# Two chained transformer blocks on one core: every second up panel multiplied as a 2 x 2 block product with seven half-size products instead of eight

## The chip, the cores and the metric

The kernel runs on one core of a Trainium2 chip. The metric is the device time of one execution in microseconds, the median over runs. A core has TensorE (matrix multiplication, called PE in the profile), VectorE (DVE), ScalarE (ACT), GpSimd (POOL) and SyncE (SP, which only issues DMAs here). They run their own programs in order and wait for each other by semaphores. TensorE writes into PSUM, which has eight banks of 512 float32 columns; VectorE and ScalarE read it from there.

## What is computed

The reference chains two blocks on x of 512 tokens and 1024 features. The first is a mixer (long convolutions and an mLSTM), cross attention and a perceptron with a squared relu. The second has two layers, each with a mixer and a gated perceptron. What the change touches are the three perceptrons (cut to that):

```python
h = h + jnp.square(jax.nn.relu(_rms_norm(h, norm_ff_g[l]) @ ff_w1[l])) @ ff_w2[l]      # "ff": 1024 -> 4096 -> 1024
...
def swiglu(x, w_gate, w_up, w_down):
    return (jax.nn.silu(x @ w_gate) * (x @ w_up)) @ w_down                             # "glu0", "glu1": 1024 -> 2816 -> 1024
```

All is float32. The kernel gets near that precision with float16 multiplications: each operand is split into a high part (rounded to float16) and a low part (the rest, as float16), and a product is the sum of high x high, high x low and low x high.

## The kernel before

Features lie on the 128 partitions and tokens in the columns. Weights come in panels of 128 x 2048 float32 (1 MB; for an up or gate matrix 8 row tiles by 256 output features). SyncE loads panel g into W[g % 2] as soon as panel g - 2 is split (semaphore panel_low). `split` runs on two engines: ScalarE writes the high half (128 x 2048, L1240), then VectorE the low half (L1822), into W16, the two homes in W_PARTS that TensorE reads in turn. `earlier` and `released` say which panel must have been multiplied before its home is written again.

A product on TensorE (`product`, L383 to L385) is three matmuls. A perceptron (`mlp`) has these stages:

- Head: the first two panels, in halves of 256 tokens (`half_panels`), while the normalization before it still works on the second half of the tokens. Their homes are in ARENA. Two more panels are split meanwhile (head_panel + 2 and + 3).
- Up panels: each later panel is 2 tiles of 128 features by 512 tokens; a tile is 8 products of 512 columns in one bank of the ring A (psum_a, four banks). In ff the panels are ("up", 2) to ("up", 15), in the glus ("gate", j) and ("up", j) for j = 1 to 10, in turn.
- After each tile ScalarE reads the bank into TS with relu or silu (`first_tiles`, L1325), VectorE makes the hidden tile in GF (`hidden`, a square at L2007 in ff, gate times up at L2004 in the glus), ScalarE its high part (`hidden_high`, L1334) and GpSimd its low part (L2644). GF and TS have room for two panels, so a tile of panel j waits for hidden_low of panel j - 2.
- Down panels: first the lower 512 output features (512 columns each), then the upper ones in halves of 256 tokens.

The ring B (psum_b, three banks) serves the norm sums and is idle during the up panels. GpSimd also multiplies x by a constant after a norm (`rescale`) for the residual.

Of the kernel before, what the change touches and what calls it, by code (L numbers as in the profile page):

```python
# [8 lines left out]
P = 128  # L9
T = 512  # L10
# [21 lines left out]
for _name, _n in ([(n, 8) for n in ("norm_mix", "norm_x", "norm_mem", "norm_ff", "final", "mix_g0", "mix_g1", "mix_b0",  # L32
# [9 lines left out]
              ("gla01", 128), ("selcol", 127), ("halfcol", 128), ("groupback", 512), ("rope_cos", 512),  # L42
              ("rope_sin", 512), ("filt_z", 512), ("decay", 2048), ("decay_b0", 512)]
# [5 lines left out]
SMALL_W1, SMALL_W2, SMALL_W3, SMALL_GATE, N_SMALL = 0, 64, 128, 2176, 2432  # L49

# [43 lines left out]
def build(nc, x_in, mem_in, weights, params, small_w, const, dft, y_out):  # L94
    with ExitStack() as ctx:
# [119 lines left out]
        G16 = parts(m.take(32 * T), 32, T)  # L215
        TS = m.take(4, T)
        GF = m.take(4, T)
        NT = Arena(8192).take(8, T)

# [7 lines left out]
        HOMES = [W16[:, 0], W16[:, 1], spare16[:, 0], spare16[:, 1], mix16w[:, 0], mix16w[:, 1], last16]  # L227
        IN_ARENA, IN_MIX, IN_LAST = (2, 3), (4, 5), 6
# [84 lines left out]
        class Mlp:  # L313


            def __init__(self, name, groups, gated, norm, next_norm):
                self.name, self.groups, self.gated, self.norm, self.next_norm = name, groups, gated, norm, next_norm
                self.ups = ("gate", "up") if gated else ("up",)
                self.head = (("gate", 0), ("up", 0)) if gated else (("up", 0), ("up", 1))
                self.later_ups = [(what, j) for j in range(groups) for what in self.ups if (what, j) not in self.head]  # L320
# [6 lines left out]
        FF = Mlp("ff", FF_GROUPS, False, "ff", "final")  # L327
        GLU0 = Mlp("glu0", GLU_GROUPS, True, "ln_mix0", "ln_ffn0")
        GLU1 = Mlp("glu1", GLU_GROUPS, True, "ln_mix1", "ln_ffn1")
# [29 lines left out]
        def _(pe):  # L359
# [21 lines left out]
            def product(out, left, right, first, last):  # L381

                nc.tensor.matmul(out, left(0), right(0), start=first, stop=False)  # L383
                nc.tensor.matmul(out, left(0), right(1), start=False, stop=False)  # L384
                return nc.tensor.matmul(out, left(1), right(0), start=False, stop=last)  # L385
# [499 lines left out]
            def mlp(M):  # L885
                half_panels([(M.name,) + key for key in M.head],
                            [lambda m, half, key=key: (M.name,) + key + (m, half) for key in M.head], IN_ARENA, U16,
                            wait=low_halves(M.norm), **second_sums(M.norm))
                for key in M.later_ups:
                    w, g = panel()  # L890
                    panel_of[(M.name,) + key] = g
                    w = w.rearrange("p l (k c) -> p l k c", k=KT)
                    for m in range(2):
                        bank = reuse(A, (M.name,) + key + (m,))
# [21 lines left out]
                for n, (key, tiles) in enumerate(M.low_steps):  # L916
                    w, g = weights(key, tiles)
                    final = n == len(M.low_steps) - 1
                    for m in range(4):
                        if n == 0:  # L920
                            banks[m] = reuse(A, (M.name, "y", m))
                        for i, kt in enumerate(tiles):
                            if m == 0:
                                pe.wait_ge(sem(f"hidden_low_{M.name}"), kt + 1)
                            last = product(banks[m][:, :], lambda l: w[:, l, i, m * P:(m + 1) * P], lambda l: G16[:, l, kt, :],
                                           n + i == 0, final and i == len(tiles) - 1)
                        if final:
                            last.then_inc(A.done, 1)
                    if not final:
                        step_done(g, last)  # L930
                    elif key != "both":
                        released[g] = A.done, A.n

# [273 lines left out]
        def _(act):  # L1207
# [37 lines left out]

            def high(ready, n, out, src, signal, bias=None):
# [1703 lines left out]
```

## Time and profile before

| | |
|---|---|
| time before, median of 3 runs (lowest, highest) | 1993.16 us (1988.92, 1994.02) |
| span of the profiled execution | 1992.6 us |
| its own time beside the span | none is shown; the span is the first to the last instruction |
| mean granted TensorE clock | 0.995 of full speed |
| TensorE busy / weight loads | 1958.3 us (98%) / 1185.2 us |
| VectorE, ScalarE, GpSimd busy | 934.0 us, 732.8 us, 345.4 us |
| chain that ended last | PE 91%, DVE 5%, the rest 1% each |
| DMA | 179.66 MB, mean 90 GB/s |

The busy time of TensorE is the union of its matmuls, whose ends are modelled (they overlap), so rates are read from the distance between starts. The chain that ended last is followed back from the last instruction to what released each.

### The profile page before, as it was taken

What the parts mean: (1) busy time and instruction counts of PE and PEld (TensorE: products, weight loads), DVE (VectorE), ACT (ScalarE), POOL (GpSimd) and SP (SyncE); (2) the same over time, 40 slices, a digit from 0 to 9 for tenths busy, and PEclk for the clock granted to TensorE, in tenths of its full rate; (3) what the DMA queues carried; (4) which work ended last, traced back from release to release, by engine and by line L of the source; (5) the groups of instructions that cost most, each with busy time, mean ns of one, the idle gap of its engine ahead of it and who ended that gap; (6) DMA issues with size and microseconds to landing.
All of it is one profiled execution on the core that took longest, in us unless ns stands there. A gap on an engine that the chain in (4) does not pass through costs nothing.

```text
span 1992.6 us, 27298 instructions
## 1 busy us (share of the span) xinstructions
PE 1958.3 (98%) x11532; PEld 1185.2 (59%) x11532; DVE 934.0 (47%) x1254; ACT 732.8 (37%) x1173; POOL 345.4 (17%) x355
## 2 busy tenths in 40 slices
PE   8999999999999999999999999999999999999997
PEld 5655655757664444885577444448775585444476
DVE  6666776655543322245755222223555663222224
ACT  6344311444343331144534322213455543223213
POOL 1011111410131210033024211200500124212001
PEclk9999999999999999999999999999999999999999
DMA  7221200233322333322221223333121023322331
GB/s 249 84 84 52 77 22 22 95 118 106 106 79 93 104 106 106 105 87 100 70 106 64 95 96 106 106 106 128 43 75 53 24 83 106 106 102 93 101 106 43
DMA packets 28228, 179.66 MB, mean 90 GB/s; under 512 B 2960, under 2 KB 7184, under 8 KB 7184
## 3 DMA queue, kind: packets, MB, share of 16 engines
q1 hardware_dynamic: 27312, 170.93, 24.9%
q10 hardware_dynamic: 512, 4.94, 0.7%
q0 software_dynamic: 288, 2.10, 0.3%
q8 instruction: 91, 1.49, 0.3%
q14 instruction: 25, 0.20, 0.0%
HBM read 175.86 MB, written 2.10 MB: 89 GB/s over the span
## 4 chain that ended last, share of the span: by engine, by line
PE 91%; DVE 5%; ACT 1%; DMA 1%; issue 1%; POOL 1%; SPq 0%; ACTq 0%; DVEq 0%
PE psum_a L383 26%; PE psum_a L384 26%; PE psum_a L385 26%; PE psum_b L520 2%; PE psum_a L726 2%; PE psum_a L662 1%; PE psum_a L737 1%; DMA W<-weights 1%; PE psum_b L639 1%; DVE ARENA L1841 1%; PE psum_a L704 1%; PE psum_a L853 1%; PE psum_b L1065 1%; PE psum_a L1019 0%; PE psum_a L1084 0%
## 5 line engine op out<-in xcount | busy, mean ns | idle before, releaser
L1822 DVE SCALAR_TENSOR_TENSOR W_PARTS<-W,W_PARTS 128x2048 f16<-128x2048 f32 x138 | 316.1, 2294 | 575.3 <-ACT W_PARTS L1240 575.1
L383 PE MATMUL psum_a<-U,W_PARTS 128*128 128x512 f16 (+1 forms) x1240 | 466.0, 376 | 2.1 <-DVE U L1836 2.1
L384 PE MATMUL psum_a<-U,W_PARTS 128*128 128x512 f16 (+1 forms) x1240 | 465.9, 376 | 0.0
L385 PE MATMUL psum_a<-U,W_PARTS 128*128 128x512 f16 (+1 forms) x1240 | 465.8, 376 | 0.0
L1240 ACT ACTIVATE W_PARTS<-W 128x2048 f16<-128x2048 f32 x138 | 262.4, 1906 | 441.9 <-PE psum_a L385 440.1
L383 PE MATMUL psum_a<-ARENA,W_PARTS 128*128 128x256 f16 (+1 forms) x860 | 268.1, 312 | 4.1 <-DVE ARENA L2339 2.3
L385 PE MATMUL psum_a<-ARENA,W_PARTS 128*128 128x256 f16 (+1 forms) x860 | 268.0, 312 | 0.0
L384 PE MATMUL psum_a<-ARENA,W_PARTS 128*128 128x256 f16 (+1 forms) x860 | 268.0, 312 | 0.0
L383 PEld LDWEIGHTS psum_a<-U,W_PARTS 128*128 128x128 f16 x1240 | 121.5, 98 | 147.5 <-issue 5.2
L385 PEld LDWEIGHTS psum_a<-U,W_PARTS 128*128 128x128 f16 x1240 | 121.5, 98 | 141.8 <-issue 1.1
L384 PEld LDWEIGHTS psum_a<-U,W_PARTS 128*128 128x128 f16 x1240 | 121.5, 98 | 141.3 <-issue 3.7
L2644 POOL TENSOR_TENSOR ARENA<-ARENA 128x512 f16<-128x512 f32 x76 | 118.2, 1575 | 452.7 <-ACT ARENA L1334 452.7
L1325 ACT ACTIVATE ARENA<-psum_a 128x512 f32<-128x512 f32 (+1 forms) x84 | 45.5, 552 | 186.1 <-PE psum_a L385 186.0
L383 PEld LDWEIGHTS psum_a<-ARENA,W_PARTS 128*128 128x128 f16 x860 | 84.2, 98 | 48.8 <-issue 2.8
L385 PEld LDWEIGHTS psum_a<-ARENA,W_PARTS 128*128 128x128 f16 x860 | 84.2, 98 | 43.4
L384 PEld LDWEIGHTS psum_a<-ARENA,W_PARTS 128*128 128x128 f16 x860 | 84.2, 98 | 43.3
L383 PE MATMUL psum_a<-MIX,W_PARTS 128*128 128x256 f16 (+1 forms) x288 | 92.2, 320 | 0.5 <-DVE MIX L1908 0.5
L384 PE MATMUL psum_a<-MIX,W_PARTS 128*128 128x256 f16 (+1 forms) x288 | 92.1, 320 | 0.0
L385 PE MATMUL psum_a<-MIX,W_PARTS 128*128 128x256 f16 (+1 forms) x288 | 92.1, 320 | 0.0
L2004 DVE SCALAR_TENSOR_TENSOR ARENA<-psum_a,ARENA 128x512 f32<-128x512 f32 (+1 forms) x48 | 30.8, 646 | 101.0 <-PE psum_a L385 101.0
L2601 POOL TENSOR_TENSOR SQ<-SQ 128x256 f32<-128x256 f32 x16 | 18.2, 1155 | 280.4 <-ACT SQ L1223 280.3
L1334 ACT ACTIVATE ARENA<-ARENA 128x512 f16<-128x512 f32 x76 | 44.7, 620 | 52.4 <-DVE ARENA L2007 46.8
(317 smaller groups left out, 2950.1 us busy)
## 6 DMA issues: line engine op xcount, KB each, us to landing
W<-weights SPq DMA_DIRECT2D x159, 1024.0 KB, 4.8
CON<-const ACTq DMA_DIRECT2D x1, 3071.5 KB, 11.5
X<-x_in SPq DMA_DIRECT2D x4, 256.0 KB, 3.9
X<-x_in SPq DMA_DIRECT2D x1, 1024.0 KB, 7.9
U<-dft POOLq DMA_DIRECT2D x1, 1024.0 KB, 5.3
ARENA<-dft POOLq DMA_DIRECT2D x1, 1024.0 KB, 5.2
U<-mem_in ACTq DMA_DIRECT2D x1, 1024.0 KB, 4.8
y_out<-U SPq DMA_DIRECT2D x2, 512.0 KB, 2.9
```

The costliest lines, as they stand in the source:

```text
L383: nc.tensor.matmul(out, left(0), right(0), start=first, stop=False)
L384: nc.tensor.matmul(out, left(0), right(1), start=False, stop=False)
L385: return nc.tensor.matmul(out, left(1), right(0), start=False, stop=last)
L520: last = nc.tensor.matmul(bank[:, 0:HALF], ones, square_tile(kt), start=kt == 0, stop=kt == KT - step)
L639: nc.tensor.matmul(bank[:, :], QK[:, 4 + h, j * P:(j + 1) * P], QK[:, h, :], start=True, stop=True).then_inc(B.done, 1)
L726: last = nc.tensor.matmul(bank[:, :], FDFT[:, part, odd, n, kt * P:(kt + 1) * P], sources[part][:, 2 * odd + n, :], start=n == 0, stop=n == 1)
L1240: nc.scalar.activation(HOMES[home_of[g]][:, 0, :], W[g % 2][:, :], ACT.Copy, scale=W_SCALE).then_inc(sem("panel_high"), 1)
L1325: nc.scalar.activation(TS[:, 2 * (j % 2) + m, cols], A.bank(key)[:, 0:cols.stop - cols.start], ACT.Silu if M.gated else ACT.Relu, scale=DE ...
L1334: nc.scalar.activation(G16[:, 0, 2 * j + m, :], GF[:, 2 * (j % 2) + m, :], ACT.Copy).then_inc(sem(f"hidden_high_{M.name}"), 1)
L1822: nc.vector.scalar_tensor_tensor(out=home[:, 1, :], in0=W[g % 2][:, :], scalar=W_SCALE, in1=home[:, 0, :], op0=ALU.mult, op1=ALU.subtract) ...
L2004: nc.vector.scalar_tensor_tensor(out=g, in0=A.bank(up)[:, 0:n], scalar=DESCALE, in1=ts, op0=ALU.mult, op1=ALU.mult).then_inc(A.freed_sem(u ...
L2644: nc.gpsimd.tensor_tensor(G16[:, 1, n, :], GF[:, n % 4, :], G16[:, 0, n, :], ALU.subtract)\
```

## The change

In `mlp` the later up panels go in pairs: a plain panel, multiplied as before, and one by seven products. In ff the pairs are (2, 3), (4, 5) to (14, 15), 7 in all; in each glu (gate j, up j) for j = 1 to 10. For the second of a pair the panel is taken as 2 x 2 blocks A (output tile m by even or odd row tiles), and the input as 2 x 2 blocks (even or odd row tiles by first or second half of the tokens). The seven products are a form of Strassen's scheme. Each is 4 x 3 matmuls of 128x256, into 256 columns of a psum_b bank:

- q1 (A11 x B11), q6, q7 and q4 accumulate one after another in psum_b0; q5 and q3 in psum_b2; q2 (A12 x B21) in psum_b1.
- The order is q1, q5, q2, q6, q3 (`first_five`), then the next plain panel's tile 0, q7 (`sixth`), its tile 1, q4 (`seventh`), and the next q1. After the last pair q7 and q4 stand behind the first two down tiles.
- Between the accumulations the running sums are read: q1, q5 and q1 + q6 by ScalarE (`read_part` 0, 1, 2 into SQ), and with them VectorE adds the three quarters of the two output tiles (`add_part` 0 after q2, 1 after q3, 2 after q7). The fourth quarter is psum_b0 after q4, read by ScalarE in ff (`tile_21`) and by VectorE in the glus (in `finish`).

The combined operands are made on chip. Once for each perceptron VectorE makes four combinations of the input, 128x1024 each (`v_made`), split into high (ScalarE, `v_high`) and low parts (VectorE, `v_low`). For each panel it makes four sums of 128x512 (`block_sums`), and the seven blocks are split in three steps (`raw` 1024 columns, `sums` 1536, `rest` 1024), instead of one split of 2048. The host orders the columns of those panels by blocks. The second panel that was split under the head is now one of these, so one is left there; the glu heads' homes move from 12288 to 1536 in ARENA, where the blocks now need room; and `rescale` starts after v_made.

The diff, cut:

```diff
             def mlp(M):
+                def one_of_seven(name):
+                    block, right = source[name]
+                    opens = name in ("q1", "q5", "q2")
+                    for i in range(4):
+                        last = product(out_of[name][:, 0:HALF], lambda l: M.blocks[:, l, block, i, :], lambda l: right(l)[:, i, :],
+                                       opens and i == 0, i == 3, not opens)
+                    last.then_inc(sem("seven_done"), 1)
+
+                def first_five(key):
...
+                    pe.wait_ge(sem("blocks_low"), 2 * n + 1)
+                    if n:
+                        pe.wait_ge(sem("tile_21"), n)
+                    one_of_seven("q1")
+                    pe.wait_ge(sem("blocks_low"), 2 * n + 2)
+                    pe.wait_ge(sem("v_low"), 4 * MLPS[M.norm] + 4)
+                    if n:
+                        pe.wait_ge(sem("tile_added"), 3 * n - 1)
+                    one_of_seven("q5")
+                    one_of_seven("q2")
+                    pe.wait_ge(sem("part_read"), 3 * n + 1)
+                    one_of_seven("q6")
+                    pe.wait_ge(sem("part_read"), 3 * n + 2)
+                    one_of_seven("q3")
+
+                def sixth(key):
+                    pe.wait_ge(sem("panel_low"), panel_of[(M.name,) + key] + 1)
+                    pe.wait_ge(sem("part_read"), 3 * M.seven[key] + 3)
+                    one_of_seven("q7")
+
+                def seventh(key):
+                    pe.wait_ge(sem("tile_added"), 3 * M.seven[key] + 3)
+                    one_of_seven("q4")
...
-                for key in M.later_ups:
+                for plain, seven in M.pairs:
                     w, g = panel()
...
                         last.then_inc(A.done, 1)
+                        if before:
+                            (sixth, seventh)[m](before)
                     released[g] = A.done, A.n
+                    first_five(seven)
+                    before = seven
```

ScalarE's `mlp`:

```diff
                 split(head_panel(M.norm, 2))
-                split(head_panel(M.norm, 3))
                 for j in range(1 if M.gated else 2):
                     first_tiles(M, j, 1)
+                v_high(M)
+                for j in range(1 if M.gated else 2):
                     hidden_high(M, j)
-                for j in range(1 if M.gated else 2, M.groups):
-                    first_tiles(M, j)
-                    used_panels(M, [(what, j) for what in M.ups])
-                    hidden_high(M, j)
+                before = None
+                for plain, seven in M.pairs:
+                    raw_high(M, seven)
+                    sums_high(M, seven)
+                    if before:
+                        hidden_high(M, before[1], (0,))
+                        if not M.gated:
+                            tile_21(M, before)
+                    plain_tile(M, plain, 0)
+                    rest_high(M, seven)
+                    if before:
+                        hidden_high(M, before[1], (1,))
+                    split(panel_of[(M.name,) + seven] + 1)
+                    plain_tile(M, plain, 1)
+                    for i in range(3):
+                        read_part(M, seven, i)
+                    if not M.gated:
+                        hidden_high(M, plain[1])
+                    before = seven
```

VectorE's `mlp` (`rest_high` on ScalarE waits for q4 of the panel before, `raw_high` for its q3):

```diff
                 split(head_panel(M.norm, 2))
-                split(head_panel(M.norm, 3))
+                v_made(M, X if M.gated else NT)
...
+                v_low(M)
+                block_sums(M, M.pairs[0][1])
+                before = None
+                for n, (plain, seven) in enumerate(M.pairs):
+                    if before:
+                        add_part(M, before, 1)
+                    raw_low(M, seven)
+                    if before:
+                        finish(M, before, 0)
+                    sums_low(M, seven)
+                    if before:
+                        add_part(M, before, 2)
+                        finish(M, before, 1)
+                    rest_low(M, seven)
+                    split(panel_of[(M.name,) + seven] + 1)
+                    if not M.gated:
+                        hidden(plain[1])
+                    add_part(M, seven, 0)
+                    if n + 1 < len(M.pairs):
+                        block_sums(M, M.pairs[n + 1][1])
+                    before = seven
```

On TensorE in ff, at the turn from one panel to the next. Before, the first matmuls of each bank are these, each followed by 23 more into the same bank, down three panels:

```order
L383 MATMUL psum_a2<-U,W_PARTS 128x512 [waits a_free2,panel_low]
...
L383 MATMUL psum_a3<-U,W_PARTS 128x512 [waits a_free3]
...
L383 MATMUL psum_a0<-U,W_PARTS 128x512 [waits a_free0,panel_low]
...
L383 MATMUL psum_a1<-U,W_PARTS 128x512 [waits a_free1]
...
L383 MATMUL psum_a2<-U,W_PARTS 128x512 [waits a_free2,panel_low]
```

Now, at the same place, from the second plain panel on (MIX holds the input's combinations and CON the blocks; the rows are a plain tile, q7, a plain tile, the end and the start of q4, q1, q5, q6 and q3):

```order
L422 MATMUL psum_a0<-U,W_PARTS 128x512 [waits a_free0,panel_low]
...
L422 MATMUL psum_b0<-MIX,CON 128x256 [waits part_read,panel_low]
...
L422 MATMUL psum_a1<-U,W_PARTS 128x512 [waits a_free1]
...
L422 MATMUL psum_b0<-MIX,CON 128x256 [waits tile_added]
...
L424 MATMUL psum_b0<-MIX,CON 128x256
L422 MATMUL psum_b0<-U,CON 128x256 [waits tile_21,blocks_low]
...
L422 MATMUL psum_b2<-MIX,CON 128x256 [waits tile_added,v_low,blocks_low]
...
L422 MATMUL psum_b0<-MIX,CON 128x256 [waits part_read]
...
L422 MATMUL psum_b2<-U,CON 128x256 [waits part_read]
```

Between tiles that waited for a bank four tiles old stand now products that wait for reads of the bank just written: q1 (tile_21) directly behind q4, and q6 (part_read).

ScalarE's queue for one pair in ff (the rows after hidden_high of the plain panel: raw_high, sums_high, hidden_high, tile_21 at L1487, a plain tile, rest_high, hidden_high, the next panel's split, a plain tile, and the three read_part at L1381); before, a panel had two tiles, one split and two hidden_high:

```order
L1353 ACTIVATE CON<-W0 128x1024 [waits seven_done,panel_landed0]
L1359 ACTIVATE CON<-SMALL 128x1536 [waits block_sum]
L1475 ACTIVATE ARENA<-ARENA 128x512 [waits relu_squared]
L1487 ACTIVATE ARENA<-psum_b0 128x256 [waits seven_done]
L1481 ACTIVATE ARENA<-psum_a0 128x512 [waits a_done]
L1368 ACTIVATE CON<-W0 128x1024 [waits block_sum,seven_done]
L1475 ACTIVATE ARENA<-ARENA 128x512 [waits relu_squared]
L1341 ACTIVATE W_PARTS<-W1 128x2048 [waits a_done,panel_landed1]
L1481 ACTIVATE ARENA<-psum_a1 128x512 [waits a_done]
L1381 ACTIVATE SQ<-psum_b0 128x256 [waits seven_done]
L1381 ACTIVATE SQ<-psum_b2 128x256 [waits seven_done]
L1381 ACTIVATE SQ<-psum_b0 128x256 [waits seven_done]
```

The copy of q1 stands five operations behind tile_21, all of them behind q4 of the panel before.

VectorE under the head of glu0. Before, two splits follow each other between the hidden tiles of the head's halves:

```order
L2004 SCALAR_TENSOR_TENSOR ARENA<-psum_a2,ARENA 128x256 [waits a_done,a_free0]
L1822 SCALAR_TENSOR_TENSOR W_PARTS<-W0,W_PARTS 128x2048 [waits panel_high]
L1822 SCALAR_TENSOR_TENSOR W_PARTS<-W1,W_PARTS 128x2048 [waits panel_high]
L2004 SCALAR_TENSOR_TENSOR ARENA<-psum_a1,ARENA 128x256 [waits a_done,a_free3]
L2004 SCALAR_TENSOR_TENSOR ARENA<-psum_a2,ARENA 128x256 [waits a_done,a_free0]
```

Now:

```order
L1996 SCALAR_TENSOR_TENSOR W_PARTS<-W0,W_PARTS 128x2048 [waits panel_high]
L2038 TENSOR_TENSOR ARENA<-X 128x1024 [waits gained_ln_mix0,high_ln_mix0]
L2040 SCALAR_TENSOR_TENSOR ARENA<-ARENA,X 128x1024 [waits v_made]
L2043 SCALAR_TENSOR_TENSOR ARENA<-ARENA,X 128x1024 [waits v_made]
L2047 SCALAR_TENSOR_TENSOR ARENA<-X,PAR 128x256 x4
L2281 SCALAR_TENSOR_TENSOR ARENA<-psum_a3,ARENA 128x256 [waits a_done,a_free1]
L2281 SCALAR_TENSOR_TENSOR ARENA<-psum_a0,ARENA 128x256 [waits a_done,a_free2]
L2059 SCALAR_TENSOR_TENSOR MIX<-ARENA,MIX 128x1024 [waits v_made,v_high] x4
L2005 TENSOR_TENSOR ARENA<-W1 128x512 [waits panel_landed1]
L2007 TENSOR_TENSOR ARENA<-ARENA,W1 128x512 [waits block_sum]
L2009 TENSOR_TENSOR ARENA<-ARENA,W1 128x512 [waits block_sum]
L2010 TENSOR_TENSOR W1<-W1 128x512
```

One split has gone, and v_made, v_low and the first panel's sums stand before the first raw_low, for which q1 waits.

## Rows read from the trace of the kernel before

**Rows 1.** The page, busy time, share of the span and instructions.
```profile
PE 1958.3 (98%) x11532; PEld 1185.2 (59%) x11532; DVE 934.0 (47%) x1254; ACT 732.8 (37%) x1173; POOL 345.4 (17%) x355
```
**Rows 2.** Stage table: up panels of ff and glu0, and the kernel's end.
```profile
core 0: us, PE busy (x) PEld busy (x) DVE busy (x) ACT busy (x) POOL busy (x), PEclk, DMA share, GB/s
578.90:720.50 141.60, 141.60 (x657) 64.19 (x656) 48.95 (x42) 57.14 (x69) 30.18 (x27) 1.00 0.29 98
1086.40:1293.00 206.60, 206.60 (x959) 93.71 (x958) 59.68 (x40) 58.83 (x59) 38.83 (x21) 1.00 0.30 102
...
1978.00:1992.00 14.00, 4.29 (x19) 3.15 (x17) 8.20 (x18) 6.83 (x18) 0.00 (x0) 0.85 0.37 125
```
**Rows 3.** Order in time (start, duration, us), ff, matmuls of 512 columns: 15 rows.
```profile
639.79 0.38 PE L383 MATMUL psum_a<-U,W_PARTS 128*128 128x512 f16 x1
...
642.81 0.38 PE L385 MATMUL psum_a<-U,W_PARTS 128*128 128x512 f16 x1
```
**Rows 4.** The same, matmuls of 256 columns: 26 rows, and their readers.
```profile
899.84 0.27 PE L384 MATMUL psum_a<-U,MIX 128*128 128x256 f16 x1
...
901.25 0.27 PE L385 MATMUL psum_a<-U,MIX 128*128 128x256 f16 x1
...
901.56 0.66 ACT L1273 ACTIVATE ARENA<-psum_a 128x256 f32<-128x256 f32 x2
...
902.55 0.39 ACT L1273 ACTIVATE ARENA<-psum_a 128x256 f32<-128x256 f32 x1 [0.33 <-PE psum_a L385]
902.57 0.27 PE L385 MATMUL psum_a<-U,MIX 128*128 128x256 f16 x1
```
**Rows 5.** Line L2004: durations in ns, least, median, most.
```profile
L2004 DVE SCALAR_TENSOR_TENSOR ARENA<-psum_a,ARENA x48: 406/691/694, 1069.1 to 1857.4; 128x512 f32<-128x512 f32 x40, 128x256 f32<-128x256 f32 x8
```
**Rows 6.** Order in time where TensorE waited for L2339 (0.42 us each).
```profile
399.49 0.76 DVE L2339 SCALAR_TENSOR_TENSOR ARENA<-psum_a,ARENA 128x256 f16<-128x256 f32 x2
400.03 0.10 PEld L383 LDWEIGHTS psum_a<-ARENA,W_PARTS 128*128 128x128 f16 x1 [1.21 <-issue]
400.06 0.27 PE L383 MATMUL psum_a<-ARENA,W_PARTS 128*128 128x256 f16 x1 [0.96 <-DVE ARENA L2339]
```
**Rows 7.** Order in time, head of ff: the two prepared splits.
```profile
561.56 3.71 ACT L1240 ACTIVATE W_PARTS<-W 128x2048 f16<-128x2048 f32 x2
...
563.50 4.49 DVE L1822 SCALAR_TENSOR_TENSOR W_PARTS<-W,W_PARTS 128x2048 f16<-128x2048 f32 x2 [2.83 <-ACT W_PARTS L1240]
```
**Rows 8.** Order in time, ScalarE in a panel of ff.
```profile
641.28 0.60 ACT L1325 ACTIVATE ARENA<-psum_a 128x512 f32<-128x512 f32 x1 [3.28 <-PE psum_a L385]
641.78 1.90 ACT L1240 ACTIVATE W_PARTS<-W 128x2048 f16<-128x2048 f32 x1
646.64 1.23 ACT L1334 ACTIVATE ARENA<-ARENA 128x512 f16<-128x512 f32 x2 [2.96 <-DVE ARENA L2007]
```
**Rows 9.** DMA issues, median us to landing.
```profile
W<-weights SPq DMA_DIRECT2D x159, 1024.0 KB, 4.8
```
**Rows 10.** Head of glu0: order in time, and durations of L2667 in ns.
```profile
1039.54 2.77 DVE L1902 TENSOR_TENSOR X<-X,MU 128x256 f32<-128x256 f32 x8
...
1071.18 4.49 DVE L1822 SCALAR_TENSOR_TENSOR W_PARTS<-W,W_PARTS 128x2048 f16<-128x2048 f32 x2 [1.31 <-ACT W_PARTS L1240]
...
1076.47 0.42 DVE L2004 SCALAR_TENSOR_TENSOR ARENA<-psum_a,ARENA 128x256 f32<-128x256 f32 x1 [0.46 <-PE psum_a L385]
...
1071.36 4.58 POOL L2667 TENSOR_SCALAR X<-X,PAR 128x256 f32<-128x256 f32 x1
...
L2667 POOL TENSOR_SCALAR X<-X,PAR x24: 474/476/4579, 1070.1 to 1656.9; 128x256 f32<-128x256 f32 x24
```
**Rows 11.** Order in time, head of ff: hidden tiles, GpSimd, the next reader.
```profile
567.91 1.42 DVE L2007 TENSOR_TENSOR ARENA<-ARENA 128x256 f32<-128x256 f32 x4
570.49 2.66 DVE L2007 TENSOR_TENSOR ARENA<-ARENA 128x256 f32<-128x256 f32 x4 [1.15 <-ACT ARENA L1325]
...
569.74 2.46 POOL L2644 TENSOR_TENSOR ARENA<-ARENA 128x512 f16<-128x512 f32 x2 [7.28 <-ACT ARENA L1334]
...
579.12 0.60 ACT L1325 ACTIVATE ARENA<-psum_a 128x512 f32<-128x512 f32 x1 [4.58 <-PE psum_a L385]
```

More of the change, by code:

```diff
@@ L49 @@
 SMALL_W1, SMALL_W2, SMALL_W3, SMALL_GATE, N_SMALL = 0, 64, 128, 2176, 2432
+BLOCK = 512
+A11, A12, S1, S2, S4, A22, S3 = range(7)
+V5, V6, V4, V7 = range(4)
+PRODUCTS = ("q1", "q5", "q2", "q6", "q3", "q7", "q4")
 F32 = mybir.dt.float32
@@ L313, in build, with __init__ @@
         class Mlp:
-            def __init__(self, name, groups, gated, norm, next_norm):
+            def __init__(self, name, groups, gated, norm, next_norm, hidden, blocks, sums, v32, homes, seven_before):
                 self.name, self.groups, self.gated, self.norm, self.next_norm = name, groups, gated, norm, next_norm
+                self.hidden, self.blocks, self.sums, self.v32, self.homes = hidden, blocks, sums, v32, homes
+                if gated:
+                    self.pairs = [(("gate", j), ("up", j)) for j in range(1, groups)]
+                else:
+                    self.pairs = [(("up", j), ("up", j + 1)) for j in range(2, groups, 2)]
+                self.seven = {b: seven_before + n for n, (_, b) in enumerate(self.pairs)}
                 self.ups = ("gate", "up") if gated else ("up",)
                 self.head = (("gate", 0), ("up", 0)) if gated else (("up", 0), ("up", 1))
-                self.later_ups = [(what, j) for j in range(groups) for what in self.ups if (what, j) not in self.head]
                 chunks = [(c, range(4 * c, 4 * c + 4)) for c in range(groups // 2)]
@@ L379, in panel, with product @@
                 return HOMES[home], g
[L381 to L385, printed above, removed]
+            def product(out, left, right, first, last, goes_on=False):
+                nc.tensor.matmul(out, left(0), right(0), start=first, stop=False, skip_group_check=goes_on)
+                nc.tensor.matmul(out, left(0), right(1), start=False, stop=False, skip_group_check=goes_on)
+                return nc.tensor.matmul(out, left(1), right(0), start=False, stop=last, skip_group_check=goes_on)
             def project_panel(name, q, rhs, width=T, first_wait=None, inside=None, after=None, home=None):
@@ L885, in mlp @@
             def mlp(M):
+                G16 = M.hidden
                 half_panels([(M.name,) + key for key in M.head],
-                            [lambda m, half, key=key: (M.name,) + key + (m, half) for key in M.head], IN_ARENA, U16,
+                            [lambda m, half, key=key: (M.name,) + key + (m, half) for key in M.head], M.homes, U16,
                             wait=low_halves(M.norm), **second_sums(M.norm))
-                for key in M.later_ups:
+                even, odd, first, second = slice(0, KT, 2), slice(1, KT, 2), *HALVES
@@ L928, in mlp @@
                             last.then_inc(A.done, 1)
+                        if n == 0 and m == 0:
+                            sixth(before)
+                        elif n == 0 and m == 1:
+                            seventh(before)
                     if not final:
@@ L932, in mlp @@
                         released[g] = A.done, A.n
+                pe.wait_ge(sem("tile_21"), M.seven[before] + 1)
+                pe.wait_ge(sem("tile_added"), 3 * M.seven[before] + 3)
                 wide = {}
@@ new lines, in block_low, with raw_low @@
+            def block_low(M, first, end, src, high, n, signal):
+                flat = lambda l: M.blocks[:, l, first:end].rearrange("p b k c -> p (b k c)")
+                dve.wait_ge(sem(high), n)
+                nc.vector.scalar_tensor_tensor(out=flat(1), in0=src, scalar=W_SCALE, in1=flat(0), op0=ALU.mult, op1=ALU.subtract)\
+                    .then_inc(sem(signal), 1)
+            def raw_low(M, key):
+                n, g = M.seven[key], panel_of[(M.name,) + key]
+                block_low(M, A11, A12 + 1, W[g % 2][:, 0:2 * BLOCK], "blocks_high", 2 * n + 1, "blocks_low")
@@ L2783, in _down_panels, with _by_blocks, _seven_from @@
     return low + both + high
+def _by_blocks(panel):
+    w = panel.reshape(P, 4, 2, 2, P)
+    return _np.concatenate([w[:, :, k, m].reshape(P, BLOCK) for m, k in ((0, 0), (0, 1), (1, 1), (1, 0))], 1)
+def _seven_from(panels, first):
+    return [_by_blocks(w) if n >= first and n % 2 else w for n, w in enumerate(panels)]
 def _swiglu_panels(gate, up, down):
-    return [w for pair in zip(_panels_k8(gate), _panels_k8(up)) for w in pair] + _down_panels(down)
+    return _seven_from([w for pair in zip(_panels_k8(gate), _panels_k8(up)) for w in pair], 3) + _down_panels(down)
 def _weight_stream(a):
```

223 lines of the change are left out of this document (191 added, 32 removed).

## The prediction

> **What bounds the kernel now.** I read the page first, for the engine that sets the end; then stage tables for the three stretches of up and gate panels, where the change lies; then the order in time inside them. TensorE is busy 98% of the span [rows 1]. In the stretch of a perceptron in which whole panels of 512 columns follow one another (ff and glu0 are shown, glu1 is like glu0), its busy time equals the stretch to the last digit, while VectorE and ScalarE are busy less than half of it [rows 2]. Nobody is waited for there: only work taken from TensorE shortens the stretch, and whatever makes TensorE wait lengthens it by the full wait.
>
> **What the change removes.** A plain panel is 48 matmuls of 512 columns. They start 0.2157 us apart (14 steps in 3.02 us, [rows 3]): 10.35 us. A panel by seven products is 7 x 12 = 84 matmuls of 256 columns. The new ones are not in the trace, but others of that width are, and start 0.1092 us apart (25 steps in 2.73 us, [rows 4]): 9.17 us. Saved: 1.18 us a panel and, for 7 + 10 + 10 = 27 panels, **31.9 us**. Not an eighth of 27 x 10.35 = 279 (34.9), since each matmul has a small cost of its own that is now paid more often.
>
> **What it adds on TensorE's path, in the steady pairs.** I put t = 0 at the end of q4's slot, the last product of the previous seven, which accumulates in psum_b0.
>
> *q4 to q1.* The next product, q1, overwrites psum_b0, so it waits for whoever reads q4's result (tile_21), and nothing stands between them. A reader starts 0.31 us after the last 256-column matmul has started (901.25 to 901.56, [rows 4]), 0.20 after its slot. A VectorE read of 256 columns from PSUM takes 0.41 at least [rows 5]. From the end of such an operation (399.49 + 0.42) to the next matmul of a TensorE that waited for it are 0.14 us (400.06, [rows 6]). Together 0.75 us. ScalarE reads q4 in the ff perceptron. It falls in every pair but the first of each perceptron, 24 times: **18.0 us**. One of its 256-column reads alone takes 0.39, two in a row 0.66, so the second adds 0.27 [rows 4]. Bounds: 0.51 (0.20, a read of 0.27 and hardly any release) to 0.86, so 12 to 21 us.
>
> *q1 to q6.* q6 accumulates on q1 in the same bank and waits until ScalarE has copied q1 (read_part 0). Between them stand q5 and q2. With the wait above q2's slot ends at 0.75 + 36 x 0.1092 = 4.68. The copy stands in ScalarE's queue behind work that itself waits for q4. Spacings there: 2048 columns 1.81 (two in 3.71, [rows 7]), 512 columns 0.50 to 0.55 (641.28 to 641.78, and two in 1.23, [rows 8]), 256 columns 0.27; on the line between 512 and 2048, 1024 columns cost 0.96. In glu0 and glu1 it is: start 0.20, rest_high 0.96, hidden_high 0.55, the next panel's split 1.81, plain_tile 0.50, the copy 0.39: 4.41, and 4.55 with the release. That is 0.13 before TensorE arrives: nothing is lost, narrowly. In ff tile_21 (0.27) and a plain_tile (0.50) stand ahead as well: 5.32, so TensorE waits 0.64 us in 6 pairs: **3.8 us**. Bounds: 0, if one of these is shorter; 0.5 more in each of the 24 pairs (12 us), if each of the queued operations costs its duration instead of its spacing.
>
> *Covered edits.* The other waits have room. A panel lands 4.8 us after its issue [rows 9]; rest_low ends at 2.5 in glu (3.3 in ff), so the next blocks land at 7.5 to 8 and their first four sums run in 7.5 to 11.5. raw_low ends by 13 and sums_low by 15.5, against a need at 20.3 or later. add_part 2 is wanted by q4 at 19, and ready at 14.5 to 16. The plain panel's low half is written at 5.9 to 6.7 and wanted at 7.3 to 8. VectorE's new operations per pair (3584 columns of low halves, four sums, three partial tiles) bring its work to about 13 of some 20 us. If any of it is late, q4's wait for add_part 2 comes first: that cover is 3 to 4 us.
>
> **A port that two engines want.** VectorE operations with two operands in SBUF and GpSimd operations lengthen each other here: GpSimd's 128x256 operation, 0.476 us in the median, took 4.58 while two splits ran on VectorE [rows 10], and four VectorE multiplications took 2.66 us beside GpSimd against 1.42 alone [rows 11]. In a steady pair GpSimd needs 4 x 1.2 us (two in 2.46, [rows 11]) and VectorE some 11 us with two such operands: 16 of 20, so it holds. It costs in the start below. The Trainium skill has this as a rule (SBUF — State Buffer, "Who interferes with whom"): a VectorE instruction with two SBUF inputs contends with a GpSimd instruction that reads SBUF, and whoever issues first keeps the port for the whole instruction. The rows agree. Without that rule, with no delay of the sums, the start would cost 5.5 us less in all.
>
> **The start of each perceptron.** Before, the second prepared panel is split under the head and nobody waits. Now v_made, v_low, the sums and raw_low stand on VectorE before q1. In glu0, in the times of the old trace: the first split ends at 1073.45 (half of the two from 1071.18, [rows 10]); three 1024-column operations at 1.15 and four of 256 at 0.4 end at 1078.5 (1024 columns from 0.346 a 256-column operation, eight in 2.77, and 2.25 a split); two hidden tiles 1079.25; v_low four times 1.13 with a first wait of 0.3 gives 1084.1. The sums are chained by semaphores, 0.65 each, and GpSimd's rescale, which now runs there, enters the two gaps at 0.65 on average: the third ends 1087.35, the fourth 1088.0, raw_low 1089.1. TensorE ends the head at 1076.27 (the reader starts 1076.47, [rows 10]) and the plain panel at 1086.6: it waits 2.6 us for q1, and 0.4 more for sums_low before q5. That is 3.0, and 3.0 in glu1. In ff the head ends at 568.55 (the reader at 579.12, less 0.2 and one panel, [rows 11]). The split ends 565.75 [rows 7], v_made 570.35, eight hidden halves 573.05, v_low 577.6, the sums, with GpSimd's 1.2 us tiles in both gaps, 582.6, raw_low 583.7; TensorE's plain panel ends at 578.9: 4.8 + 0.4 = 5.2 us. Together **11.2 us**; without GpSimd in the gaps 5.7, with every operation held once 14.
>
> **Sum.** 31.9 - 18.0 - 3.8 - 11.2 = -1.1 us: the wins are spent. The profile's own span is 1992.6; no other time of that execution is shown, and the median of the runs is 1993.16, 0.6 above it. I take the median plus 0.8, **1994.0 us**.
>
> **Rivals.** A measurement of this kernel can tell some 0.3%, or 6 us.
> - *Faster.* The starts and q6's wait are hidden (ScalarE and VectorE as quick as their shortest rows, GpSimd kept out of the gaps) and the turnaround is 0.65: 31.9 - 15.6 - 2 = 14 us, 1979. For it: I priced 1024 columns by a line between other sizes, and three starts from one pattern. Against it: the turnaround is a chain of three rows. Half-way cases lie within 6 us. Chance beyond 6 us: 0.20.
> - *Slower: q6 waits in all 24 pairs.* The margin in glu is 0.13 us. If the five queued ScalarE operations cost 0.1 us more each, glu loses 18 x 0.37 = 6.7 and ff 3.0 more: 2004. It decides from about 0.3 us over the queue as a whole. Chance 0.18.
> - *Slower: VectorE is late.* If the port makes a pair's VectorE work longer than its 3 to 4 us of cover, q4 waits. One us in each of 24 pairs gives 2018. The 4 us in hand speak against it. Chance 0.06.
> - *The clock.* TensorE ran at 2.4 GHz (granted 1.00) in those stretches, and the grant fell only where it was busy 4.29 of 14 us (0.85, [rows 2]). New gaps of 0.75 in 20 us are far from that. If a fifth of the 27 pairs ran at 1.2 GHz, 5 x 20 = 100 us would be added: 2094. Chance 0.03. The Trainium skill warns of it (TensorE: Matmul & The Clock Gate, "A second HAM failure mode: psum-queue depth-cycling"): short idle moments between groups while PSUM banks are cycled made the clock alternate. No row here shows that.
> - *As summed*, within 6 us of no change: 0.53.
>
> **How the numbers follow.** Faster is the first rival, 0.20; slower the next three, 0.27; same 0.53. The range leaves out the far part of the faster case (below 1984), the late VectorE, the clock and the far part of the ScalarE case (above 2003), 2 in 10 together. The sum's own range, from the middle of its bounds, is 1987 to 1999.
>
> **What would show it.** In the profile after: (1) matmuls of the products 0.109 us apart, 84 in 9.17 us; (2) 24 gaps of 0.75 us on TensorE released by L1487 in ff and L2090 in glu; (3) gaps near 0.6 before q6 in ff, released by L1381, and none in glu; (4) 3 to 5 us of waiting in each start, released by L2016; (5) no waits for add_part or landing; (6) clock 1.00. I am wrong if (2) is under 0.5 or (4) under 1 us, or if (3) shows in glu.

## The result, and the profile after

The changed kernel takes 1997.13 us (median of 16 runs, 1994.36 to 1998.22) against 1992.38 us for the kernel before (16 runs beside it, 1988.89 to 1996.20). The ratio is 1.0018 with a 95% interval of 1.0011 to 1.0025: slower, by 2 to 5 us, and within the 0.3% that the prediction called no change. The forecast was 1994.0, which is 0.8 above the median that it started from; the measured difference is 3.6 us by the ratio and 4.7 by the medians. The profiled execution took 1997.98 us with a span of 1996.2; the span of before was 1992.6.

The busy line of the page, as [rows 1]:

```profile
PE 1936.5 (97%) x12504; PEld 1279.8 (64%) x12504; DVE 1137.3 (57%) x1547; ACT 805.4 (40%) x1313; POOL 377.2 (19%) x355
```

TensorE has 972 matmuls more, and its busy time is 22 us less. (It is not 31.9 less: the busy time also counts a modelled end at each new gap, and some matmuls ran at a lower clock, as shown below.) The span did not get shorter, so TensorE waits more. The stage table shows where, as [rows 2]; the rows are the start of ff, its second pair, the other five of ff, glu0 from its second pair on with the first down panels behind, and the kernel's end:

```profile
core 0: us, PE busy (x) PEld busy (x) DVE busy (x) ACT busy (x) POOL busy (x), PEclk, DMA share, GB/s
578.90:606.79 27.89, 22.14 (x132) 14.11 (x132) 20.78 (x19) 10.53 (x14) 9.32 (x6) 0.88 0.21 76
606.79:627.55 20.76, 19.86 (x132) 12.77 (x132) 14.14 (x15) 9.85 (x15) 6.35 (x4) 1.00 0.29 102
627.55:731.30 103.75, 99.33 (x661) 63.98 (x662) 67.29 (x71) 49.47 (x71) 33.93 (x21) 1.00 0.32 112
1115.70:1320.00 204.30, 198.88 (x1290) 125.61 (x1291) 108.01 (x124) 80.08 (x101) 34.54 (x19) 1.00 0.30 109
1977.86:1991.86 14.00, 7.64 (x29) 5.46 (x26) 8.79 (x20) 6.49 (x18) 0.00 (x0) 0.88 0.22 75
```

Before, TensorE's busy time equalled each such stretch. Now it lacks 0.90 of 20.76 us in a pair of ff, and the first row lacks 5.75 and ran at a granted clock of 0.88. (The busy time counts a matmul's modelled end, so a gap seen from start to start is a little longer.) TensorE's waits from the start of ff to the end of glu0 (us in total, times, longest):

```profile
PE psum_b L422 <- DVE CON L2016: 6.2, 1, 6.2
PE psum_b L422 <- DVE ARENA L2090: 5.5, 9, 0.6
PE psum_b L422 <- ACT ARENA L1487: 3.4, 6, 0.6
PE psum_b L422 <- ACT SQ L1381: 2.0, 6, 0.3
PE psum_b L422 <- DVE ARENA L2016: 1.9, 2, 1.5
```

The first is the start of ff and the last the start of glu0: q1 and q5 waiting for the first low halves. The second (glu0) and the third (ff) are q1 waiting for the reader of q4, the fourth is q6 waiting for the copy of q1. In the order in time (start, duration) they look like this, first in ff, then in glu0, then q6 in ff:

```profile
606.46 0.27 PE L424 MATMUL psum_b<-MIX,CON 128*128 128x256 f16 x1
606.77 0.38 ACT L1487 ACTIVATE ARENA<-psum_b 128x256 f32<-128x256 f32 x1 [7.21 <-PE psum_b L424]
607.30 0.27 PE L422 MATMUL psum_b<-U,CON 128*128 128x256 f16 x1 [0.56 <-ACT ARENA L1487]
...
1135.98 0.42 DVE L2090 SCALAR_TENSOR_TENSOR ARENA<-psum_b,ARENA 128x256 f32<-128x256 f32 x1 [5.33 <-PE psum_b L424]
1136.55 0.27 PE L422 MATMUL psum_b<-U,ARENA 128*128 128x256 f16 x1 [0.61 <-DVE ARENA L2090]
...
611.12 0.27 PE L424 MATMUL psum_b<-U,CON 128*128 128x256 f16 x1
611.72 0.28 PE L422 MATMUL psum_b<-MIX,CON 128*128 128x256 f16 x1 [0.33 <-ACT SQ L1381]
```

From 606.46 to 607.30 are 0.84 us where 0.109 would do: a gap of 0.73 (0.77 in the glus). From 611.12 to 611.72 are 0.60: 0.49. The start of ff, with VectorE, GpSimd and TensorE:

```profile
577.08 0.68 DVE L2005 TENSOR_TENSOR SMALL<-W 128x512 f32<-128x512 f32 x1
577.79 1.53 DVE L2007 TENSOR_TENSOR SMALL<-SMALL,W 128x512 f32<-128x512 f32 x1
...
580.80 1.64 DVE L2010 TENSOR_TENSOR W<-W 128x512 f32<-128x512 f32 x1
582.36 2.17 DVE L2016 SCALAR_TENSOR_TENSOR CON<-W,CON 128x1024 f16<-128x1024 f32 x1
...
572.94 10.52 POOL L2940 TENSOR_TENSOR ARENA<-ARENA 128x512 f16<-128x512 f32 x4 [11.13 <-ACT ARENA L1475]
...
578.06 0.38 PE L424 MATMUL psum_a<-U,W_PARTS 128*128 128x512 f16 x1
584.59 0.40 PE L422 MATMUL psum_b<-U,CON 128*128 128x256 f16 x1 [6.16 <-DVE CON L2016]
584.78 0.42 PE L423 MATMUL psum_b<-U,CON 128*128 128x256 f16 x1
```

TensorE waits 6.31 us for the first raw_low (from start to start 6.53, less 0.216 for a matmul of 512 columns); in each glu the same way 1.66 and then 0.55. Three of the four sums take 1.5 to 1.6 us where the first takes 0.68. And when TensorE goes on, 24 matmuls come 0.213 us apart (584.59 to 589.47), at a granted clock of 0.50, 1.2 GHz; only then they are 0.109 apart.

To compare kernels stage by stage I take the distance between the reciprocals (L1990, "RECIPROCAL RINV") of the second half of one norm and the first half of the next; a perceptron lies between them. Before and after: ff 321.35 and 329.17 us, glu0 337.18 and 334.49, glu1 337.17 and 334.49.

### The profile page after: what moved, and what is told of

Same layout as the page of the kernel before. It is cut to its first block, busy times and chain, and to the rows that moved or that the text cites. A ratio compares the mean times of both kernels' runs of the same rounds, so it can differ in the third digit from the quotient of the medians.

```text
span 1996.2 us, 29878 instructions
## 1 busy us (share of the span) xinstructions
PE 1936.5 (97%) x12504; PEld 1279.8 (64%) x12504; DVE 1137.3 (57%) x1547; ACT 805.4 (40%) x1313; POOL 377.2 (19%) x355
## 4 chain that ended last, share of the span: by engine, by line
PE 86%; DVE 8%; ACT 3%; issue 2%; DMA 1%; POOL 1%; SPq 0%; ACTq 0%; DVEq 0%
PE psum_a L422 21%; PE psum_a L424 21%; PE psum_a L423 21%; PE psum_b L422 4%; PE psum_b L424 4%; PE psum_b L423 4%; PE psum_b L559 2%; PE psum_a L765 2%; ACT W_PARTS L1341 1%; DVE ARENA L2118 1%; PE psum_a L701 1%; PE psum_a L776 1%; DMA W<-weights 1%; PE psum_b L678 1%; DVE MIX L2059 1%
## 5 line engine op out<-in xcount | busy, mean ns | idle before, releaser
L1996 DVE SCALAR_TENSOR_TENSOR W_PARTS<-W,W_PARTS 128x2048 f16<-128x2048 f32 x111 | 254.6, 2296 | 300.7 <-ACT W_PARTS L1341 300.6
L1341 ACT ACTIVATE W_PARTS<-W 128x2048 f16<-128x2048 f32 x111 | 211.0, 1904 | 277.6 <-PE psum_a L424 272.7
L422 PE MATMUL psum_a<-U,W_PARTS 128*128 128x512 f16 (+1 forms) x808 | 302.8, 375 | 1.6 <-DVE U L2113 1.6
L423 PE MATMUL psum_a<-U,W_PARTS 128*128 128x512 f16 (+1 forms) x808 | 302.4, 374 | 0.0
L424 PE MATMUL psum_a<-U,W_PARTS 128*128 128x512 f16 (+1 forms) x808 | 302.3, 374 | 0.0
L2940 POOL TENSOR_TENSOR ARENA<-ARENA 128x512 f16<-128x512 f32 x76 | 135.6, 1792 | 406.3 <-ACT ARENA L1475 406.3
L424 PEld LDWEIGHTS psum_a<-U,W_PARTS 128*128 128x128 f16 x808 | 79.4, 98 | 91.2 <-issue 1.4
L422 PEld LDWEIGHTS psum_a<-U,W_PARTS 128*128 128x128 f16 x808 | 79.4, 98 | 91.0 <-issue 5.2
L423 PEld LDWEIGHTS psum_a<-U,W_PARTS 128*128 128x128 f16 x808 | 79.4, 98 | 85.5 <-issue 4.0
L422 PE MATMUL psum_b<-MIX,ARENA 128*128 128x256 f16 x320 | 87.2, 273 | 0.8 <-DVE ARENA L2016 0.8
L423 PE MATMUL psum_b<-MIX,ARENA 128*128 128x256 f16 x320 | 87.2, 273 | 0.0
L424 PE MATMUL psum_b<-MIX,ARENA 128*128 128x256 f16 x320 | 87.2, 273 | 0.0
L422 PE MATMUL psum_b<-U,ARENA 128*128 128x256 f16 x240 | 65.4, 272 | 14.0 <-DVE ARENA L2090 11.0
```

The costliest lines, as they stand in the source:

```text
L1341: nc.scalar.activation(HOMES[home_of[g]][:, 0, :], W[g % 2][:, :], ACT.Copy, scale=W_SCALE).then_inc(sem("panel_high"), 1)
L1996: nc.vector.scalar_tensor_tensor(out=home[:, 1, :], in0=W[g % 2][:, :], scalar=W_SCALE, in1=home[:, 0, :], op0=ALU.mult, op1=ALU.subtract) ...
L2940: nc.gpsimd.tensor_tensor(M.hidden[:, 1, n, :], GF[:, n % 4, :], M.hidden[:, 0, n, :], ALU.subtract)\
```

## The experiments

All are edits of the changed kernel; the ratios are to the kernel before. The profiles decide here more than the medians: a perceptron that an edit leaves alone repeats to some hundredths of a microsecond, a median only to some 2 us. The medians of all seven fell by 1.3 to 3.3 us more, against the changed kernel's 1997.13, than their three perceptrons did; part of that is the clock in other stretches (see E3 and the sum at the end).

**E1, the bank behind q4 (e1_two_banks).**

```diff
+        def sum_bank(n):
+            return psum_den if n % 2 else psum_b[0]
...
-                    if n:
-                        pe.wait_ge(sem("tile_21"), n)
-                    one_of_seven("q1")
+                    if n > 1:
+                        pe.wait_ge(sem("tile_21"), n - 1)
+                    one_of_seven("q1", n)
```

> Edit: q1, q6, q7 and q4 of a panel go in turn into psum_b0 and into the eighth bank, which is idle in the perceptrons, so q1 waits for tile_21 of the panel before last. Time counted from the end of q4's slot. Theory (the wait behind q4 is real, but ScalarE's queue behind q4 stands right after it): the 24 gaps of 0.73 to 0.78 us before q1 go, and q6 then waits for the copy of q1, which still ends at 5.15 in ff and 4.45 in the glus, while TensorE arrives at 3.93. In ff the gap before q6 grows from 0.49 to about 1.2 and nothing is won; in each glu pair a gap of 0.5 comes up and 0.77 goes, 0.25 x 18 = 4.5 us. In all about 4.5 us less than the changed kernel, some 1992.5. Rival (the turnaround is a loss of its own, and the ScalarE queue has room): all 18.3 us come back, some 1979.

Measured: 1990.49 us (11 runs; before 1993.13; ratio 0.9989, 0.9980 to 0.9999). ff is 329.28, no shorter than 329.17; glu0 331.78, 2.71 less. TensorE in ff, the last matmul of q4, the first of q1, and then the turn from q2 to q6:

```profile
604.32 0.27 PE L428 MATMUL psum_b<-MIX,CON 128*128 128x256 f16 x1
604.42 0.27 PE L426 MATMUL psum_den<-U,CON 128*128 128x256 f16 x1
...
608.24 0.27 PE L428 MATMUL psum_b<-U,CON 128*128 128x256 f16 x1
609.57 0.28 PE L426 MATMUL psum_den<-MIX,CON 128*128 128x256 f16 x1 [1.06 <-ACT SQ L1386]
...
606.85 1.91 ACT L1346 ACTIVATE W_PARTS<-W 128x2048 f16<-128x2048 f32 x1
608.65 0.60 ACT L1486 ACTIVATE ARENA<-psum_a 128x512 f32<-128x512 f32 x1
609.12 0.39 ACT L1386 ACTIVATE SQ<-psum_den 128x256 f32<-128x256 f32 x1
```

The gap before q1 is gone (0.10 from start to start) and the one before q6 has grown from 0.49 to 1.22: the same 1.22 us, at another place. The copy (609.12) stands behind the split (606.85). In the glus 0.77 goes and 0.46 comes. So most of the 18.3 us of turnaround are not a loss of their own: they covered a wait for ScalarE's queue that shows as soon as they are gone.

**E2, the copy ahead of the split (e2_copy_first).** ScalarE:

```diff
                         hidden_high(M, before[1], (1,))
+                    read_part(M, seven, 0)
                     split(panel_of[(M.name,) + seven] + 1)
                     plain_tile(M, plain, 1)
-                    for i in range(3):
+                    for i in (1, 2):
```

> Edit: ScalarE copies q1 (read_part 0) before the split of the next plain panel, not after it and a plain tile. Theory: the 0.49 us gap before q6 goes in 6 pairs of ff, 2.9 us; in the glus there is none to take. The plain panel's split comes 0.38 later, ready 7.1 after q4's slot in ff against a need at 7.3, and 6.3 against 7.3 in the glus: no new wait. About 2.9 us less than the changed kernel, some 1994. Rival (the 0.49 us is made by something else, such as q5 or q2 waiting): no change. A price of the delayed split would show as a wait for panel_low before the plain panel.

Measured: 1992.89 us (11 runs; ratio 0.9998, 0.9989 to 1.0007). ff is 326.24, 2.93 less, and its gaps before q6 are gone; the glus are unchanged at 334.48. As expected to the tenth.

**E3, both (e3_both).** The diffs of E1 and E2 together.

> Edit: the two edits of the experiments with the alternating bank and the early copy together. Theory (two waits that cover one another): the gap before q1 (0.73 and 0.77) goes and none comes up before q6. The next bound is the plain panel's low half: in ff it is ready 7.1 us after q4's slot against a need at 6.55, so 0.6 comes back there, in the glus 6.3 against 6.55. Gain against the changed kernel: ff 6 x (0.73 + 0.49 - 0.6) = 3.8, glus 18 x 0.77 = 13.9, together 17.7 us, far more than the sum of the two apart (7.4); some 1979, under the kernel before by 13. Rival (the waits are independent): the sum of the two apart, whatever they give.

Measured: 1975.69 us (5 runs, 1974.19 to 1977.59; ratio 0.9916, 0.9902 to 0.9929). ff is 324.58 (4.59 less), glu0 327.57 (6.92 less), glu1 the same: 18.4 us, where the two alone gave 5.3 and 2.9. The turn from q4 to q1 in glu0 and the reader of q4:

```profile
1130.23 0.27 PE L428 MATMUL psum_b<-MIX,ARENA 128*128 128x256 f16 x1
1130.34 0.27 PE L426 MATMUL psum_den<-U,ARENA 128*128 128x256 f16 x1
...
1130.54 0.42 DVE L2096 SCALAR_TENSOR_TENSOR ARENA<-psum_b,ARENA 128x256 f32<-128x256 f32 x1 [4.55 <-PE psum_b L428]
```

The read now runs beside q1. In ff small gaps stay, 0.18 before q3 and 0.24 before the plain tile, where I had expected 0.6. The 17.7 expected became 18.4. The profiled span fell by more, 22.8: 1.7 of that is the clock in the last norm (below), and 2.6 lie in the mixer between glu0 and glu1, which the edit does not touch. There too the low clock fell on other matmuls: the granted clock was 0.50 from 1525.0 to 1531.6 in the changed kernel, and in E3 from 1504.5 to 1507.7 and from 1552.3 to 1555.5.

**E4, GpSimd held back in ff (e4_pool_held).** GpSimd:

```diff
                 pool.wait_ge(sem("v_made"), 4 * MLPS[M.norm] + 4)
+                if M is FF:
+                    pool.wait_ge(sem("blocks_low"), 2)
```

> Edit: in ff GpSimd starts its first hidden low halves only when the first raw and sums blocks are split, so that nothing of GpSimd runs beside the first block sums. Theory (port contention makes most of the start of ff): the sums take 0.7 us each and not 1.5, raw_low 1.2 and not 2.2, and q1 of the first pair comes some 4 us earlier: the wait falls from 6.3 to about 2 us. With the shorter idle the clock stays up, and the 2.5 us of half-speed matmuls go too. About 6.5 us less than the changed kernel, some 1990.5. Rival (the combinations and their low halves, v_made and v_low, are the start's cost): the wait stays above 5 us and the time within 1.5 us of the changed kernel.

Measured: 1990.19 us (12 runs; ratio 0.9983, 0.9974 to 0.9991). VectorE and TensorE in the start:

```profile
578.43 0.69 DVE L2007 TENSOR_TENSOR SMALL<-SMALL,W 128x512 f32<-128x512 f32 x1
...
579.76 0.68 DVE L2010 TENSOR_TENSOR W<-W 128x512 f32<-128x512 f32 x1
580.37 1.22 DVE L2016 SCALAR_TENSOR_TENSOR CON<-W,CON 128x1024 f16<-128x1024 f32 x1
...
581.64 0.40 PE L422 MATMUL psum_b<-U,CON 128*128 128x256 f16 x1 [2.57 <-DVE CON L2016]
```

The sums are back at 0.69 us and raw_low at 1.22, and the wait fell from 6.31 to 2.73 (2.95 from start to start): GpSimd's work beside them cost 3.58 us. The Trainium skill's rule (SBUF — State Buffer, "Who interferes with whom") fits with these rows. The second term of the expectation was wrong: the clock fell after the 2.73 us as well, for 16 matmuls and not for 24, so 0.85 came back and not 2.5. ff is 324.74, 4.43 less.

**E5, TensorE kept busy in the wait (e5_filler).**

```diff
                     released[g] = A.done, A.n
+                    if M is FF and not before:
+                        for n in range(27):
+                            nc.tensor.matmul(psum_b[1][:, :], w[:, 0, 0, 0:P], U16[:, 0, 0, :], start=True, stop=True)
                     first_five(seven)
```

> Edit: in ff, TensorE multiplies 27 more matmuls of 512 columns into an unused bank (results not used) between the first plain panel and q1, 5.8 us of the 6.3 us in which it waited for raw_low. Theory (TensorE's own idleness before q1 made the clock fall): q1 starts when it did, but its matmuls run 0.109 us apart and not 0.213, so that the 2.5 us lost after the wait come back; ff is shorter by 2.5 us. Rival (the clock falls there for another reason, or the 0.213 us come from a weight or operand port that is busy): the first 24 matmuls of q1 and q5 stay at 0.213 us apart and ff keeps its length.

Measured: 1992.83 us (11 runs; ratio 1.0003, 0.9994 to 1.0012), and ff 327.10, 2.07 less although TensorE does 27 matmuls more. The stretch behind the wait, in this kernel:

```profile
584.59:588.00 3.41, 3.00 (x26) 2.47 (x27) 3.41 (x4) 2.13 (x3) 0.00 (x0) 1.00 0.02 5
```

and in the changed kernel:

```profile
584.59:588.00 3.41, 3.41 (x17) 2.43 (x18) 3.41 (x3) 1.91 (x3) 0.00 (x0) 0.50 0.00 0
```

The granted clock is 1.00 against 0.50 with VectorE busy for all 3.41 us in both: it was TensorE's own idleness that lowered it. The 0.4 us short of 2.5 are a wait for sums_low (0.35) that q5 now meets, since q1 ends earlier.

**E6, two low halves later (e6_late_v).** VectorE's order and TensorE's waits:

```diff
-                v_low(M)
+                v_low(M, (V5, V6))
...
                     split(panel_of[(M.name,) + seven] + 1)
+                    if n == 0:
+                        v_low(M, (V4, V7))
...
-                    pe.wait_ge(sem("v_low"), 4 * MLPS[M.norm] + 4)
+                    pe.wait_ge(sem("v_low"), 4 * MLPS[M.norm] + 2)
```

(q7 now waits for all four.)

> Edit: of the four low halves of the input's combinations VectorE makes only the two that q5 and q6 use before the first block sums; the other two (q4's and q7's) come after the first split of the next plain panel. Theory (the starts are VectorE's queue, operation after operation): 2.3 us less ahead of raw_low. In each glu the waits of 1.65 and 0.55 us go, 2.2 each; in ff the wait before q1 falls by 2.3, perhaps more if the sums then escape some of GpSimd's tiles. Together 6.7 us or more less than the changed kernel, some 1990. Rival (the sums wait for something else, such as the panel's landing or GpSimd): the waits stay.

Measured: 1988.09 us (11 runs; ratio 0.9981, 0.9971 to 0.9990). The start of ff on TensorE:

```profile
578.15 0.38 PE L424 MATMUL psum_a<-U,W_PARTS 128*128 128x512 f16 x1
582.42 0.28 PE L422 MATMUL psum_b<-U,CON 128*128 128x256 f16 x1 [3.89 <-DVE CON L2017]
```

In the glus the waits at the start are gone (332.25 each, 2.24 less); in ff the wait is 4.05, 2.26 less, and ff is 326.14, 3.03 less (the other 0.7 are seven slow matmuls fewer). Together the three are 7.5 us shorter. What VectorE has queued before the first raw_low sets the starts: two operations fewer there shorten each by their length.

**E7, all four edits (e7_all_four).** E1, E2, E4 and E6 together.

> Edit: the alternating bank, the early copy, the held GpSimd and the late two low halves together. Theory: 17.7 to 21 us of steady gaps, 4.4 us of ff's start by GpSimd, and of what is left 2.2 in each glu and 2.3 in ff with its clock (0.9): some 1964 us, 1.5% under the kernel before, with a wait of under 1 us at each start, and TensorE at full clock through each perceptron's up panels. Rival (with GpSimd's first tiles later and VectorE's two low halves behind, the pairs that follow are late): waits for hidden_low, add_part or the plain panel's low half appear in the first two pairs and eat the gain of the starts; then some 1975.

Measured: 1966.93 us (4 runs, 1966.18 to 1968.44; ratio 0.9876, 0.9860 to 0.9892), 1.2% faster than the kernel before. glu0 and glu1 are 325.34 each, 9.2 less than the changed kernel and 11.8 less than before; ff 320.55, 8.6 less and 0.8 less. In ff the expectation's terms (3.8 of gaps, 4.4 and 3.2 of the start) make 11.4; it got 3 us less, by the rival's mechanism. VectorE, GpSimd and TensorE in ff:

```profile
582.52 3.29 DVE L2003 SCALAR_TENSOR_TENSOR W_PARTS<-W,W_PARTS 128x2048 f16<-128x2048 f32 x1 [0.99 <-ACT W_PARTS L1347]
585.74 4.27 DVE L2066 SCALAR_TENSOR_TENSOR MIX<-ARENA,MIX 128x1024 f16<-128x1024 f32 x2
...
580.53 8.39 POOL L2951 TENSOR_TENSOR ARENA<-ARENA 128x512 f16<-128x512 f32 x4 [18.67 <-DVE CON L2023]
...
599.61 0.41 DVE L2078 SCALAR_TENSOR_TENSOR ARENA<-psum_b,SQ 128x256 f32<-128x256 f32 x1
...
600.08 0.28 PE L426 MATMUL psum_b<-MIX,CON 128*128 128x256 f16 x1 [2.36 <-DVE ARENA L2078]
```

GpSimd's four tiles, held back, now lie beside the split (3.29, alone 2.29) and the two late low halves (4.27, 2.35 in E6); add_part 2 is late, and q4 waits 2.5 us for it, with 16 slow matmuls behind. The start's wait is down to 0.8. Part of what E4 and E6 won was only moved: q1 starts at 578.79 here, against 581.64 in E4 and 582.42 in E6, but add_part 2 stands at 599.61, against 599.64 and 599.24. In E4 and E6 alone TensorE came too late to wait for it.

## Why the prediction was right

It was right in its mechanism and close in its sum, with one term missing. By its steps:

- *Saving, 31.9.* Confirmed. The glu pairs take 20.30 us with a gap of 0.77; 19.53 without it is 10.35 + 9.17. Where nothing waits (E3, E7) it all arrives.
- *q4 to q1, 18.0.* Measured 6 x 0.73 + 18 x 0.77 = 18.3: the start 0.20 after the slot, the read 0.38 or 0.42, the release 0.14. The chain of three rows held. E1 shows what the prediction did not say: taken away alone, this wait gives back 2.7 us in each glu and nothing in ff, for the wait for ScalarE's queue comes up in its place.
- *q1 to q6, 3.8.* Measured 6 x 0.49 = 2.9 in ff and none in the glus; E2 took exactly that. Each queued operation costs its spacing, not its duration: from tile_21 to the copy the starts are 0.28, 0.48, 0.95, 0.52, 1.80 and 0.47 apart, priced at 0.27, 0.50, 0.96, 0.55, 1.81 and 0.50. By E1 the copy is ready 0.31 us before TensorE needs it in a glu (0.77 - 0.46), where I had 0.13: the rival in which q6 waits in all pairs was further off than its margin said.
- *Starts, 11.2.* Measured 6.31 + 2.2 + 2.2 = 10.7. The total is close because two errors cancel: ff was priced at 5.2 against 6.31, each glu at 3.0 against 2.2. In ff the contention also stretched raw_low (2.17 for 1.22), and q5's 0.4 did not appear beside the slow q1; in the glus rescale stretched the last three sums only to 0.77 to 0.88. E4 puts ff's contention at 3.6 us; with some 0.45 in each glu (an estimate from those three sums against 0.69 each) that is 4.5 where 5.5 was priced. E6 puts the rest at VectorE's queue.
- *The clock, 0.* This term was missing. The prediction looked for the clock in the pairs' gaps of 0.75 us, where it stayed at 1.00, and did not ask what a wait of 5 us at the start would do, though it had forecast that wait and had [rows 2] with a clock of 0.85 where TensorE idles. It also took those rows for the only place: the trace of before has another in the middle of dense work, with the clock at 0.50 for over 6 us behind one idle time of 1.78 us. The term costs 2.5 us here; E5 shows the cause. In before:

```profile
1518.25 0.40 PE L383 MATMUL psum_a<-ARENA,W_PARTS 128*64 128x512 f16 x1 [1.78 <-DVE MU L2454]
...
1520.20:1526.80 6.60, 6.60 (x20) 3.32 (x21) 1.28 (x5) 0.81 (x1) 0.00 (x0) 0.50 0.01 2
```

- *Covered edits.* No wait for a landing, add_part or the plain panel's low half in any steady pair: right. The cover is thin, as E7 shows where GpSimd's tiles fell on it.

Sum as measured: 31.9 - 18.3 - 2.9 - 10.7 - 2.5 = -2.5 us, against -1.1 forecast; the stages give 7.82 - 2.69 - 2.68 = +2.45. The errors of the three waits (0.3 too little, 0.9 and 0.5 too much) took back 1.1 of the missing 2.5, so a part of the closeness is luck. And the sum gives 1994.3 on 1993.16; the 0.8 taken in place of 1.1 has no reason given.

The profiled spans differ by 3.6. Besides the 2.45, 1.7 are the last norm: 12.42 us between its two reciprocals before, 14.11 after, with the granted clock at 1.00 and 0.88 in that stretch. That is not shown to be the change's: the stretch was 14.1 also in the profiles of E2 and E6, and 12.4 in those of E1, E3, E4, E5 and E7. The first mixer, ahead of ff, took 0.7 less than before, with the low clock at other places as well. What lowers the clock in the last norm in some executions stays open, as does what else the medians' 4.7 us holds.

## What to carry to other kernels

A product with an eighth fewer multiplications gives only what its operands' preparation and its accumulators' turnaround leave: here 32 us were saved and all were spent in waits of 0.5 to 0.8 us, 24 times over, and in three starts. Waits in a row behind one event cover one another, so price the second with the first gone: one edit gave 5.3 us, the other 2.9, both together 18.4. And of every forecast wait on TensorE of a few microseconds ask what clock TensorE comes back with, and look for such a wait in the trace that you already have.

## What the runs showed of the hardware that was not expected

- TensorE's granted clock fell to 0.50 behind single waits of 2.5 to 6.3 us in the middle of dense work: 24 matmuls of 256 columns at 0.213 us after 6.31 us, 17 after 4.05, 16 after 2.73 and 16 after 2.5. After 6.31 and 2.73 the first matmul was already slow; after 4.05 and 2.5 some five and seven matmuls still came at the full rate. In the kernel before it fell behind 1.78 us of idle time. It did not fall behind gaps of 0.73 to 1.22 us repeated every 20 us. The depth-cycling case of the Trainium skill (TensorE: Matmul & The Clock Gate, "A second HAM failure mode: psum-queue depth-cycling") did not appear in those pairs, though three banks were cycled with a short idle moment each time.
- Contention lengthens both sides: VectorE's 128x512 sum 0.69 to 1.53 us and 128x1024 low half 1.22 to 2.17 beside GpSimd's four tiles, which took 10.52 us (8.25 in E6, where two of VectorE's low halves had gone from beside them). Of the 10.52 the first tile took 5.83, beside VectorE's low halves that followed one another without a wait and were not lengthened (4.62 for four, 2.35 for two in E4, where GpSimd did nothing); in the kernel before such a tile took 1.16.
